# PEER decoder layer on one core: two resident query chunks become streamed, and the ring of gathered experts grows from eight places to ten

## The reference, cut to what matters

```
def one_block(xb):                                   # 128 tokens
    q = (xb @ w_query).reshape(L, 8, 2, 128)         # 1024 -> 2048 columns
    s = einsum('lhpd,hpkd->lhpk', q, sub_keys)
    vals, idx = top_k(s, 16)                         # then the best 16 of the 16 x 16 sums
    ...
    u = expert_u[expert]                             # 128 experts per token, 1024 wide
    v = expert_v[expert]
    h = gelu(einsum('ld,lhkd->lhk', xb, u))
    return einsum('lhk,lhkd->ld', h * gate, v)
```

## Time and profile before

| | us |
|---|---|
| median of 3 runs | 3218.04 |
| lowest and highest | 3215.73, 3224.42 |
| the profiled execution | 3213.68 |
| its span, first to last instruction | 3211.9 |
| PE busy | 2422.9 (75%) |
| VectorE busy | 2240.5 (70%) |
| ScalarE busy | 1145.2 (36%) |
| POOL busy | 1180.8 (37%) |
| DMA moved | 1235.90 MB, mean 385 GB/s |

### The profile page before, as it was taken

How to read it: one execution, slowest core, us unless ns; L and a number is a source line. 1 busy time by engine, 2 the same in 40 slices (tenths; PEclk the granted TensorE clock), 3 DMA queues, 4 the chain that set the end, 5 groups by cost and what they waited for, 6 DMA issues and landing times.

```text
span 3211.9 us, 37849 instructions
## 1 busy us (share of the span) xinstructions
PE 2422.9 (75%) x11858; PEld 1351.2 (42%) x11858; DVE 2240.5 (70%) x5609; ACT 1145.2 (36%) x3500; POOL 1180.8 (37%) x1028
## 2 busy tenths in 40 slices
PE   8887788867788687877778777886777667775654
PEld 7674435424356343543336343542435334341111
DVE  5378656986578765797558965698657876578445
ACT  4123532244333533235332353234433253322222
POOL 0023452244423443234433344234432344424443
PEclk9998888879889798988989898888988889887777
DMA  8089999999999999999999999999999999989997
GB/s 337 14 334 404 420 408 402 363 397 420 413 403 397 391 420 398 391 386 405 421 386 397 394 419 402 407 383 393 418 396 404 394 395 416 399 343 361 422 421 319
DMA packets 189000, 1235.90 MB, mean 385 GB/s; under 512 B 21752, under 2 KB 21880, under 8 KB 54656
## 3 DMA queue, kind: packets, MB, share of 16 engines
q0 software_dynamic: 147456, 1073.81, 82.0%
q1 hardware_dynamic: 39168, 154.32, 12.4%
q10 hardware_dynamic: 2176, 5.36, 0.4%
HBM read 1229.21 MB, written 4.19 MB: 384 GB/s over the span
## 4 chain that ended last, share of the span: by engine, by line
PE 34%; DMA 25%; DVE 24%; issue 7%; ACT 7%; POOL 3%; DVEq 0%; POOLq 0%; SPq 0%; ACTq 0%
DMA ring<-in_uv,expert_used 23%; PE expert_sum L987 14%; DVE ring L1810 10%; PE bank L611 8%; POOL ring L538 3%; PE bank L592 3%; PE bank L600 2%; ACT diag L1307 2%; PE bank L618 2%; DMA chunk<-in_weights 1%; DVE arena L1448 1%; DVE arena L1758 1%; DVE arena L1761 1%; ACT h_raw L1300 1%; DVE oT L1828 1%
## 5 line engine op out<-in xcount | busy, mean ns | idle before, releaser
L538 POOL DMA_INDIRECT ring<-in_uv,expert_used x1024 | 1180.6, 1153 | 2000.9 <-PE expert_sum L987 1524.8
L987 PE MATMUL expert_sum<-ring,diag 128*64 128x512 f32 x4096 | 1221.2, 726 | 681.6 <-ACT diag L1307 680.7
L1810 DVE CUSTOM_DVE_ANT_0 ring<-ring,x_pair 128x1024 f32<-128x1024 f32 x1024 | 1230.4, 1223 | 573.4 <-DMA ring<-in_uv,expert_used 568.6
L987 PEld LDWEIGHTS expert_sum<-ring,diag 128*64 128x64 f32 x4096 | 313.0, 157 | 1331.0 <-issue 1316.2
L1300 ACT ACTIVATE h_raw<-h_raw 128x2 f32<-128x2 f32 x512 | 104.4, 204 | 1488.9 <-DVE h_raw L1810 1488.4
L1307 ACT ACTIVATE diag<-const,h_raw 128x64 f32<-128x64 f32 x1024 | 292.8, 333 | 1.1 <-PE expert_sum L987 1.1
L1303 ACT ACTIVATE h_raw<-h_raw,gate_used 128x1 f32<-128x1 f32 x1024 | 245.7, 287 | 16.7
L611 PEld LDWEIGHTS bank<-oT,chunk 128*128 128x128 f32 x1376 | 156.4, 192 | 22.7 <-issue 22.7
L611 PE MATMUL bank<-oT,chunk 128*128 128x128 f32 x1376 | 162.4, 277 | 0.0
L1448 DVE MAX8 arena<-arena 128x8 f32<-128x128 f32 (+1 forms) x384 | 103.7, 325 | 41.3 <-ACT arena L1258 36.1
L618 PEld LDWEIGHTS bank<-arena 128*128 128x128 f32 x768 | 96.3, 202 | 56.0 <-issue 51.5
(11 more groups left out here) (271 smaller groups left out, 2650.8 us busy)
## 6 DMA issues: line engine op xcount, KB each, us to landing
chunk<-in_weights SPq DMA_DIRECT2D x228, 512.0 KB, 9.3
ring<-in_weights SPq DMA_DIRECT2D x16, 1024.0 KB, 18.5
ring<-in_uv,expert_used POOLq DMA_INDIRECT x1024, 11.2
chunk<-in_weights SPq DMA_DIRECT2D x5, 1024.0 KB, 10.4
x<-in_x SPq DMA_DIRECT2D x8, 512.0 KB, 13.4
out<-oT ACTq DMA_DIRECT2D x8, 512.0 KB, 9.2
o_cat<-in_xT SPq DMA_DIRECT2D x7, 512.0 KB, 14.7
xT_even<-in_xT SPq DMA_DIRECT2D x4, 512.0 KB, 10.0
```

The lines of the kernel that those rows point to most:

```text
L538: pool.indirect_dma_start(out=ring[:, (j % RING) * 2 * D:(j % RING + 1) * 2 * D], out_offset=None, in_=io["uv"], in_offset=bass.IndirectOf ...
L987: mm = pe.matmul(expert_sum[i][c * SPAN:(c + 1) * SPAN, :], diag[:, (j % DIAGS) * SPAN:(j % DIAGS + 1) * SPAN], ring3[:, j % RING, D + i * ...
L1810: dve.tensor_tensor_reduce(u, u, x_pair[:, (j % 2) * D:(j % 2 + 1) * D], 1.0, 0.0, ALU.mult, ALU.add, h_raw[:, j:j + 1]).then_inc(dotted.s ...
```

## The change

`KEPT` and the tile `kept` are gone. All 23 chunks are streamed, so q2 and q5 are loaded again for each of blocks 1 to 7, as four half loads in each block. The 16 KB become two more places of the ring, so that the memory used is the same. 128 slots aren't a multiple of ten, so the place and the semaphore count of a slot now follow from n * 128 + j, counted over all blocks.

```diff
-RING = 8
+RING = 10
...
-KEPT = (IN_CHUNKS + OUT_CHUNKS + 2, IN_CHUNKS + OUT_CHUNKS + 5)
-STREAMED = [c for c in range(CHUNKS) if c not in KEPT]
+STREAMED = list(range(CHUNKS))
 EARLY = 2 + RING * 2 * D // (KT * W)
...
     for _c in range(IN_CHUNKS + OUT_CHUNKS, CHUNKS):
-        _use(_c, [_n], _n > 0 and _c not in KEPT)
+        _use(_c, [_n], _n > 0)
...
-        kept = sb("kept", len(KEPT) * KT * W)
...
+        def place(n, j):
+
+            r = (n * SLOTS + j) % RING
+            return ring[:, r * 2 * D:(r + 1) * 2 * D]
+
+        def arrived(n, j):
+
+            return gathered[(n * SLOTS + j) % RING], 16 * ((n * SLOTS + j) // RING + 1)
...
                 for c in range(IN_CHUNKS + OUT_CHUNKS, CHUNKS):
-                    if c not in KEPT:
-                        for half in range(2):
-                            load(LOAD_OF[c, n + 1, half])
+                    for half in range(2):
+                        load(LOAD_OF[c, n + 1, half])
...
-                    pool.wait_ge(*added.at(n, ring_free(j)))
-                    gather(j)
+                    pool.wait_ge(*added.at(n, j - RING + 1))
+                    gather(n, j)
...
             def half_there(c, m, half):
-                if c in KEPT:
-                    if m == 0:
-                        pe.wait_ge(kept_in[KEPT.index(c)], 16)
-                elif m == 0:
+                if m == 0:
...
                     for j in (2 * q, 2 * q + 1):
-                        pe.wait_ge(*gathered[j % RING].at(n, arrived(j)))
+                        pe.wait_ge(*arrived(n, j))
```

More of the change, by code:

```diff
@@ L282, in build @@
         late_in = sem("late_in")
-        kept_in = [sem(f"kept_in{i}") for i in range(len(KEPT))]
         early_in = [sem(f"early_in{i}") for i in range(EARLY)]
@@ L369, in build @@
         late_gates = signal("late_gates", 1)
-        gathered = [signal(f"gathered{i}", 16 * len(range(i, SLOTS, RING))) for i in range(RING)]
+        gathered = [sem(f"gathered{i}") for i in range(RING)]
         dotted = signal("dotted", SLOTS)
@@ L394, in build @@
         vrows = v_rows[:, :].rearrange("p (s c) -> p s c", s=2)
-        ring3 = ring[:, :].rearrange("p (r c) -> p r c", r=RING)
+        def place(n, j):
[3 more added lines that the diff above has]
+            return gathered[(n * SLOTS + j) % RING], 16 * ((n * SLOTS + j) // RING + 1)
         A_ROT, A_T = 16, 10
@@ L427, in build @@
         setup, late = 16 * 8, 16 * 2
-        def kept_chunk(c):
-            i = KEPT.index(c)
-            return kept[:, i * KT * W:(i + 1) * KT * W]
         def early_place(s):
@@ L469, in _ @@
                     sp.dma_start(x1[:, :], io["x"][0]).then_inc(x_loaded.sem, 16)
-                if c in KEPT:
-                    sp.dma_start(kept_chunk(c), io["weights"][c]).then_inc(kept_in[KEPT.index(c)], 16)
-                    continue
                 s = STREAMED.index(c)
@@ L531, in gathers, with gather @@
                         alone(pool)
-                    pool.wait_ge(*added.at(n, ring_free(j)))
-                    gather(j)
-            def gather(j):
+                    pool.wait_ge(*added.at(n, j - RING + 1))
+                    gather(n, j)
+            def gather(n, j):
                 alone(pool)
                 pool.indirect_dma_start(
-                    out=ring[:, (j % RING) * 2 * D:(j % RING + 1) * 2 * D], out_offset=None, in_=io["uv"],
+                    out=place(n, j), out_offset=None, in_=io["uv"],
                     in_offset=bass.IndirectOffsetOnAxis(ap=expert_used[:, j:j + 1], axis=0),
-                ).then_inc(gathered[j % RING].sem, 16)
+                ).then_inc(arrived(n, j)[0], 16)
             pool.wait_ge(*staged.at(0, 1))
@@ L546, in _ @@
                 pool.wait_ge(*used(max(c for s, c in enumerate(STREAMED) if s % EARLY == 2 + j), 0))
-                gather(j)
+                gather(0, j)
             gathers(0, RING)
@@ L564, in half_of @@
                 ks = slice(half * KT // 2, (half + 1) * KT // 2)
-                if c in KEPT:
-                    return kept_chunk(c).rearrange("p (k c) -> p k c", k=KT)[:, ks, :]
                 if m == 0:
@@ L988, in experts @@
                                            diag[:, (j % DIAGS) * SPAN:(j % DIAGS + 1) * SPAN],
-                                           ring3[:, j % RING, D + i * 512:D + (i + 1) * 512],
+                                           place(n, j)[:, D + i * 512:D + (i + 1) * 512],
                                            start=(q == 0), stop=(q == PAIRS - 1), tile_position=(0, c * SPAN))
@@ L1807, in experts @@
                     for j in (2 * q, 2 * q + 1):
-                        dve.wait_ge(*gathered[j % RING].at(n, arrived(j)))
-                        u = ring3[:, j % RING, 0:D]
+                        dve.wait_ge(*arrived(n, j))
+                        u = place(n, j)[:, 0:D]
                         dve.tensor_tensor_reduce(u, u, x_pair[:, (j % 2) * D:(j % 2 + 1) * D], 1.0, 0.0, ALU.mult, ALU.add, h_raw[:, j:j + 1]).then_inc(dotted.sem, 1)
```

1 line of the change is left out of this document (removed).

## The result

| | before | changed |
|---|---|---|
| median of 4 runs, us | 3217.05 | 3179.01 |
| lowest and highest | 3215.73, 3224.42 | 3177.57, 3179.84 |
| span of the profiled execution | 3211.9 | 3175.8 |

The ratio is 0.9884, with a 95% interval from 0.9871 to 0.9897: 38 us faster, a small gain but clear of the noise. The forecast was 3219 in a range from 3194 to 3254, so the time lies outside the range, and on the side that had 0.29.

The account below looks back on a forecast made before the run. It took the DMA engines as the bound, with VectorE setting the pace in part of each block. 7 x (8.0 - 5.1) = +20.3, DeltaNet stops -9.5 and start -7.4 gave +3.4 us: 3219 us, range 3194 to 3254.

Parts of the forecast that it names:

- the price of the ring: Two more gather places: 5.1 us gained per VectorE-bound stretch, seven stretches, plus 9.5 us of stops around DeltaNet.
- the query stage: PE waits for streamed chunks q2 to q7 and ends the stage 8.3 us late, taken as 8 us a block.
- VectorE sets the pace: From new indices to the end of the front, VectorE, busy 119.6 of 130 us, bounds and the ring fills.
- two gathers further ahead, and no more: In a VectorE-bound stretch, two more places let the DMA engines run 5.1 us longer before they run dry.
- the indices come when they did: At the turn to a new block, gathers end neither earlier nor later, so VectorE's new indices aren't shifted.
- rest and start: Rest, each front to the next q0: -40.1 us; start, from 166 us to block 1's front: -7.4 us.
- gathers unchanged: On the DMA engines, each gather still costs 2.57 us after the change.
- The two ways of counting: Sum of delays and gains, +3.4 us, and DMA ledger of added work less filled idle time, 3.5 us, agree.
- PE isn't held up: Rival, chance 0.24: in the query stage weights get up to half the DMA time; 3201 us, or 3194.
- The two places do nothing: Rival, chance 0.10: the added ring places are freed too late to cover anything; +32.5 us, 3250.
- the weights at a third to the end: Rival, chance 0.22: weights never get the engines alone in the query stage, PE 12.7 us late; 3254 us.
- The skill's rule: Round-robin between DMA queues, read as equal turns, would give one half each; the forecast used the measured third for weights.

Follow-up runs that it names:

- e2_ring10_noload: Kernel before with ten ring places; q2 and q5 never loaded, PE multiplies with resident sub_keys instead: 3124.1 us, ratio 0.9720.
- e2c: Kernel before with eight ring places kept; q2 and q5 never loaded, PE multiplies with resident sub_keys instead: 3217.6 us, ratio 0.9999.
- e7: Ten ring places, q2 and q5 never loaded, plus ten idle PE multiplications in each query stage of blocks 1 to 7: 3170.7 us, ratio 0.9853.
- e3: Changed kernel, but the first four half loads of the first pass wait for the use of q7: 3185.1 us, ratio 0.9913.
- m1: Layer left out, gathers alone with eight, one, two, four and ten in flight: 2.51 us of engine time with four or more, 3.0 with two, 3.1 with one.
- e4: Changed kernel with query and input chunks of later blocks loaded whole, in 8 KB rows instead of 4 KB halves: 3146.6 us, ratio 0.9791.

## Why the prediction was wrong, point by point

**Where the miss lies.** The changed kernel against e2_ring10_noload gives the price of streaming with ten places, 3179.0 - 3124.1 = 55 us; the forecast had 7 x 8.0 = 56. e2 against its control e2c gives the places with the early load, 93 us; the forecast had 35.7 + 9.5 + 2.0 + 5.4 = 52.6. So the miss of 40 us is the price of the ring.

**Right in size, partly by luck: the query stage.** The forecast had PE end the stage 8.3 us late and took 8. The cut gives 61.0 / 7 = 8.7. Timeline of PE in the query stage of block 3, after (what stands in brackets is the wait before the row), to be held against the earlier trace rows:

```profile
1268.88 1.16 PE L592 MATMUL bank<-oT,chunk 128*128 128x128 f32 x8
1270.50 2.94 PE L592 MATMUL bank<-oT,chunk 128*128 128x128 f32 x24 [0.46 <-DMA chunk<-in_weights]
1275.56 1.16 PE L592 MATMUL bank<-oT,chunk 128*128 128x128 f32 x8 [2.12 <-DMA chunk<-in_weights]
1279.36 5.28 PE L592 MATMUL bank<-oT,chunk 128*128 128x128 f32 x24 [2.63 <-DMA chunk<-in_weights]
...
1289.38 7.41 PE L592 MATMUL bank<-oT,chunk 128*128 128x128 f32 x64
...
1301.55 7.41 PE L592 MATMUL bank<-oT,chunk 128*128 128x128 f32 x64
...
1312.23 1.94 PE L968 MATMUL expert_sum<-ring,diag 128*64 128x512 f32 x8 [0.32 <-ACT diag L1288]
```

PE waits 0.46 + 2.12 + 2.63 us, for q2 and q3, none for q5, where the forecast had the worst. What the brackets don't show is the clock: the row of 24 records at 1279.36 takes 5.28 us where the equal one at 1270.50 takes 2.94. Windows of the stage, then of two pieces of it, and of the stage before:

```profile
1255.77:1314.10 58.33, 52.12 (x354) 39.35 (x353) 31.72 (x100) 15.00 (x46) 16.14 (x17) 0.94 0.99 393
1270.50:1277.40 6.90, 4.10 (x32) 3.72 (x32) 6.68 (x25) 0.00 (x0) 1.13 (x2) 1.00 1.02 416
1277.50:1284.20 6.70, 4.84 (x22) 4.85 (x23) 6.04 (x19) 0.00 (x0) 0.00 (x0) 0.50 1.02 418
```
```profile
1279.50:1330.50 51.00, 48.98 (x354) 36.80 (x352) 32.87 (x102) 15.20 (x46) 15.29 (x15) 1.00 1.00 395
```

Behind the wait of 2.12 us, and while the one of 2.63 runs, the granted clock falls from 2.4 to 1.2 GHz (1.00 to 0.50); from 1284.3 on it is 2.4 again. Of the 7.3 us by which this stage is longer, 4.2 are idle time of PE and 3.1 the same instructions running longer. In all seven stages PE spends 37.5 us at the lower level, where before it spent none; at half speed that costs some 19 us, an estimate, of the 61.0. The forecast had the whole delay as waits for chunks, 8 us a block, and they are 6.0; the clock, which it doesn't have, made up the rest. SP's issues and the two queues' shares, against the earlier trace rows:

```profile
1258.81 38.41 SPq L484 DMA_DIRECT2D chunk<-in_weights  x12
```
```profile
q0 software_dynamic: 1231, 8.92, 65.3%
q1 hardware_dynamic: 1176, 4.29, 33.0%
```

Twelve half loads in place of eight, at 33.0% of the engines: the third held. The 10.7 us at the turn-over were forecast as "near 11".

**Wrong: "VectorE sets the pace" in the pass, and "two gathers further ahead, and no more".** This is the step that failed, the price of the ring: 5.1 us for each stretch with the stops and the start, 47 us (52.6 with the early load), where e2 against e2c measures 93. It gave the pass no gain at all, as though VectorE had its floor there in the earlier trace rows. It had not. In block 3 there was little to wait for, but I had looked at block 3 alone; waits of VectorE in the same stretch behind the turn-over of block 1 in the old kernel, 568 to 678:

```profile
DVE ring L1810 <- DMA ring<-in_uv,expert_used: 7.6, 7, 1.9
```

After, the same stretch of block 1 (561 to 663), like that of block 3, has none but the turn-over's:

```profile
DVE oT L1809 <- PE expert_sum L968: 10.7, 1, 10.7
```

In the six blocks the pass took 105 to 110 us before and takes 102 to 104 with ten places, in the changed kernel, in e2 and in e7: that is close to VectorE's floor, and 28 us lay above it. In the six passes together VectorE stands idle 56.4 us before and 30.5 after.

**Right within 1 us: "the indices come when they did".** After, POOL's timeline in the query stage of block 3 reads:

```profile
1270.99 0.94 POOL L524 DMA_INDIRECT ring<-in_uv,expert_used  x1 [0.30 <-issue]
1287.30 1.07 POOL L524 DMA_INDIRECT ring<-in_uv,expert_used  x1 [15.37 <-PE expert_sum L968]
1288.68 0.94 POOL L524 DMA_INDIRECT ring<-in_uv,expert_used  x1 [0.30 <-issue]
1298.71 1.17 POOL L524 DMA_INDIRECT ring<-in_uv,expert_used  x1 [9.09 <-PE expert_sum L968]
```

The first gather for the new block goes out at 1298.71, 42.9 us after q0, where it was 1325.77 - 1279.50 = 46.3. Block 3 is the extreme: in the mean of blocks 1 to 7 it is 44.4 us after q0, and was 45.4. So PE's lateness doesn't hold up the indices, and the gathers of the new block start 9.7 us further ahead of the pass than they did. Little of the lateness is paid back by that: in e7, 60.2 us of it in the query column cost 54.5 us of the span.

**Undersized: rest and start.** Rest -49.7 in place of -40.1, start -13.8 in place of -7.4. In the start I gave 5.4 us to the early load and 2.0 to the places; by e3 the first was about right, 3 to 6, and the places have 8 to 11.

**Wrong: the price of DMA time, a term put at nothing.** The forecast held a gather fixed at 2.57 us ("gathers unchanged"), and took a dry engine as costing only its gaps. The records of the packets split the 97.8 us between the spans of e2c and e2: 45.8 us less packet time, 46.4 us less idle time of the engines after 166 us, and 5.7 before it. The idle time is about what the forecast's 47 us were made of; the packet time isn't in it. m1 shows that a restart costs time that the share counts as busy, and the slow packets' excess fell by 46 us. In the changed kernel the packets cost 14 us more in all (3053 to 3067 us), not 37.9: 34 more for the weights, nearly as forecast, and 20 less for the gathers. The two ways of counting that "agreed" in the forecast shared the error: the ledger came to +3.5 because its idle term was made from the same 5.1. It was no check.

**The rivals.** "PE isn't held up" had the direction and the lower end of the range, 3194, with the wrong reason: PE is held up. "The two places do nothing" is refuted by e2. The slower rival, the weights at a third to the end, fails as well, and its trigger didn't come about: in block 3 the last old gather is issued at 1288.68 and the first new one at 1298.71, and in every block 8.9 us or more lie between the two. With PE late, POOL waits 15.37 us for a place (above), the gather queue runs low even before that gap, and the weights get more. The two queues from 1284 to 1300 of the changed kernel:

```profile
q0 software_dynamic: 402, 2.88, 47.4%
q1 hardware_dynamic: 686, 2.47, 45.2%
```

That is why q4 to q7 came in time. The bound of the range failed because every case took 6.5 us of idle time a stretch, or less, as all there was to win. The earlier trace rows could have warned: VectorE's waits for gathers, 568.6 us, were far more than that. With six, eight and ten places they are 930.0, 556.1 and 411.3 us, so they fall by 374 and 145 us where the time falls by 316 and 93. They bound the gain from above here; they don't give it.

**The skill's rule.** With rows of 4 KB the weights get a third beside gathers with rows of 8 KB, and above; with rows of 8 KB they get half (e4). The records of the packets show why. They don't name their engine, but a record starts a few ns after another ends, and chained by that the rows of the two queues alternate one by one: 180 of 190 neighbours in the 4 us of e4 above are of different queues. So each queue gets a turn of one row, and the bytes go by the row's size. The Trainium skill, page "DMA: Bandwidth & Descriptors", section "Queues, rings and completion order", has engines drain a whole packet, typically of some 9 to 17 descriptors, before they switch. The round robin agrees with these traces; turns of 9 rows or more don't show in them, nor turns of equal length, as the rival read it. The forecast said that the page gives no sizes: it gives none in bytes or time, but it gives this count.

## What to carry to other kernels

Before a ring between a DMA stream and several engines is sized by the idle share of the DMA engines, look at how long the consumer waits for data: here a share of 0.98 hid 93 us, half of it in packets that counted as busy. When a resident tile is given up for depth, first look whether the engine that reads it is on the path in that stage; here most of the price was its lateness, and a part of that lateness was the clock that fell while it waited. Longer rows in the loads bought back 32 us. And a second count that uses the same assumption as the first is no check.

## What was not expected of the hardware

- A gather that starts on idle engines takes them 3.1 us in place of 2.51 (m1: 161 GB/s at a share of 0.48, against 422 at 1.01), so the busy share hides a part of what a dry queue costs.
- With two waits of PE of 2.12 and 2.63 us in the query stage of block 3 the granted clock falls to 0.50 for 6.8 us, and the multiplications in that stretch take nearly twice as long (5.28 us for 24 in place of 2.94). The stage of the kernel before has no such wait and reads 1.00.
- Beside a busy gather queue, the share of another queue follows the length of its rows: 33% with 4 KB against 8 KB, 53.0% with 8 KB against 8 KB, one row at a turn.
- Ring depth is worth 316 us from six to eight places and 93 from eight to ten (3 to 6 of them the early load). Whether twelve would give more isn't known; there was no memory for them.
